# A two-layer decoder step: its head by halves of the weight units, and the second layer's gate on two pairs of banks

## The chip, the cores and the metric

One core of one Trainium2 chip runs the whole program. The metric is the device time of one execution in microseconds (us), as the median of several runs. The profile is of one further execution.

## The reference

One inference step of a decoder with two layers, D_MODEL 1024, on 1024 prompt tokens and 32 sample tokens (8 sequences of 4), 1056 in all. All arithmetic is float32. What matters here:

```python
h = rms_norm(x, g);  z = h @ W_in                    # layer 0: 12 tiles of 128 columns, layer 1: 14
# layer 0: windowed attention (12 query heads, 4 kv heads); layer 1: gating in chunks of 128 tokens
u, v = split(gelu(z[:, :1536]));  vn = rms_norm(v, v_norm)
mixed = einsum('gij,ncjgd->ncigd', tril(W_s), vn) + b_s      # 4 groups of 192 columns
o = u * mixed
xo = memory_attention(rms_norm(z_q), mem_k, mem_v)   # both layers: 4 heads into 256 memory tokens
x = x + concat([o, xo]) @ W_out
x = x + (silu(causal_conv3(h2 @ W_g)) * (h2 @ W_u)) @ W_down    # h2 = rms_norm(x), D_FF 2816
```

## The kernel before

**Products.** Activations lie with features on the 128 partitions and the 1056 tokens along the free axis, in 3 chunks of 352 (`NCH`, `CH`). Each float32 product is made of three: a tensor is cut into a high part that TensorE reads at its fast float32 rate, and a low part that is the remainder. Per contraction tile k, `products` (L600 to L602) issues hi·hi, hi·lo and lo·hi. A weight **unit** is 128 x 1024 floats (512 KB), 8 tiles of k. It is loaded into `raw` by SyncE, ScalarE makes the high part `w_hi` (`high_front`, `high_up`, at L1150), and VectorE (`low_front`, L1650) or GpSimd (`low`, L468) makes the low part `w_lo`. A chunk of a unit is 24 matmuls and ends in `proj`. The chunks of even units go to banks 0 to 2 of PSUM, those of odd units to 3 to 5. Banks 6 and 7 are for small sums. Whoever reads a chunk out of PSUM counts up `freed[slot]`, on which TensorE waits before it overwrites the bank.

**The head** (layer 0, before the first attention). SyncE issues in this order (L416 to L426): unit 0, tiles 0 to 3 of x for chunk 0, the gains, tiles 4 to 7 of x for chunk 0, unit 1, all of x for chunk 1, all of x for chunk 2, ten small constants, the memory tokens, `sel_t`. The normalisation is applied behind the product: TensorE multiplies x times gain, and `rb`, the reciprocal root of the mean square of each token spread over all partitions, multiplies the result on its way out of PSUM (L2016). ScalarE makes `h_hi` (`high_of_h`, L1202) in 24 pieces e (chunk e//8, tile e%8), VectorE makes `h_lo` (L1610). `X_LANDS` names the pieces ahead of which both wait for a load of x. At piece 8 ScalarE waits for the load of chunk 1, and only then takes the high part of unit 1 (L1226 to L1230). Then ScalarE squares x in 24 instructions (L1234). TensorE (`front`, L702) makes the six chunks of units 0 and 1 in the order `FRONT_X`, with sums of squares (`x_squares`, L672) behind the fourth and the fifth. The square sum goes ScalarE root (L1188), VectorE reciprocal (L1615), TensorE spread by three small products (`norm_spread`, L650, banks 6 and 7, the third waits until `rb`'s first piece is out of bank 6), ScalarE copy to `rb`. Only then do the PSUM chunks of units 0 and 1 get read and scaled (L2016), and only then does unit 2 start. Units of the memory keys and values follow in `FRONT`, with their own normalisation (`mem_stat`, `mem_spread`, `add_mem_squares`).

**The gate** (layer 1, `gate`, L972; ScalarE L1542; VectorE L2060). It runs over 9 blocks: 32 sample tokens, then 8 chunks of 128. Per block TensorE turns the 6 tiles of vn to tokens on partitions (6 transposes, L985, into banks 0 and 1), ScalarE copies them to `vn_tok`, TensorE mixes (12 products, L1002 and L1005, into banks 2 and 3 or 4 and 5), VectorE adds the bias (L2067) and multiplies into u in `z` (L2070). TensorE's order is turn 0, turn 1, mix 0, turn 2, mix 1 and so on. There is one pair of banks for the turns, so turn n waits until ScalarE has taken turn n-1. Ahead of turn 0 TensorE waits until every column is normalised (`z_normed` 24). ScalarE's order ahead of its first copy is: high part of a weight unit, GELU of the last column tile (L1506), wait for `z_normed`, two DMA issues of the output `chunk_v` (L1538, L1539). Behind the gate TensorE waits for the last bias and then starts the memory attention (`prompt_attention`): scores (L890), on VectorE the row maximum (`top`, L1815), on ScalarE exp (L1340), and so on. VectorE first fills `q_pad` for the sample's queries (L1690). The sample's memory scores (L783) follow the first two prompt scores.

## Time and profile before

| | us |
|---|---|
| median of 3 runs | 2281.68 |
| lowest, highest | 2279.41, 2282.77 |
| the profiled execution | 2283.67 |
| its span in the trace | 2281.9 |
| mean granted TensorE clock in it | 0.996 |

A row of the timeline has the start, the duration, the engine, the line of the kernel, the instruction with its output and inputs, and in brackets how long the engine was idle before it and who released it. "x24" are that many instructions in a row. Durations of matmuls overlap, since they are pipelined, so the distance between starts is what counts. In the row of a stretch the granted clock is 1.00 for the full clock and 0.50 for half of it.

### The profile page before, as it was taken

Reading aid. Unit: us, or ns where it says so; the run is one execution under the profiler, and the core shown is the slowest. Engines: PE = TensorE matmul, PEld = TensorE weight load, DVE = VectorE, ACT = ScalarE, POOL = GpSimd, SP = SyncE. Lnnn points to the kernel's source line nnn. Section 1 sums busy time; section 2 is a strip of 40 time slices with the busy share of each in tenths; the row PEclk is TensorE's granted clock in tenths of the full one; section 3 lists DMA queues with packets and bytes.
Section 4 is the critical chain, followed back from the end, with each engine's and each line's share of the span. In section 5 each row is a group of like instructions: output and inputs, shape, how many; then the busy total and the mean of one; then the engine's idle time right before and its main releaser. Section 6 shows DMA issues by size and latency. Waiting matters only on the chain.

```text
span 2281.9 us, 38777 instructions
## 1 busy us (share of the span) xinstructions
PE 2249.3 (99%) x15074; PEld 2155.3 (94%) x15074; DVE 1126.9 (49%) x2138; ACT 663.8 (29%) x1214; POOL 552.6 (24%) x412
## 2 busy tenths in 40 slices
PE   8999999999999999999999999999999999999999
PEld 7987679999999999999999986999999999999999
DVE  5335671564454554444562236246454555454554
ACT  6323791422211222211252225243211122211121
POOL 0002453322211222211252222342211222211221
PEclk9999999999999999999999999999999999999999
DMA  4223001111111111111111121111110111111112
GB/s 170 84 101 135 22 5 47 38 56 56 46 37 37 46 55 55 43 39 37 46 51 51 47 93 37 41 46 56 50 43 28 46 55 55 46 38 36 46 55 89
DMA packets 39143, 123.39 MB, mean 54 GB/s; under 512 B 5296, under 2 KB 13456, under 8 KB 38256
## 3 DMA queue, kind: packets, MB, share of 16 engines
q1 hardware_dynamic: 34656, 112.75, 15.1%
q10 hardware_dynamic: 4400, 9.43, 1.1%
q8 instruction: 60, 0.98, 0.2%
q14 instruction: 27, 0.22, 0.0%
HBM read 115.57 MB, written 8.63 MB: 54 GB/s over the span
## 4 chain that ended last, share of the span: by engine, by line
PE 92%; DVE 3%; issue 2%; ACT 1%; POOL 1%; DMA 0%; SPq 0%; ACTq 0%; DVEq 0%; POOLq 0%
PE ps L600 28%; PE ps L601 28%; PE ps L602 28%; DVE h_lo L1610 1%; PE ps L890 1%; PE ps L923 1%; PE ps L904 1%; PE ps L1002 1%; PE ps L783 1%; ACT s_exp L1340 1%; DMA x<-in_x_t 0%; PE ps L752 0%; POOL w_lo L468 0%; PE ps L985 0%; PE ps L1005 0%
## 5 line engine op out<-in xcount | busy, mean ns | idle before, releaser
L600 PE MATMUL ps<-h_hi,w_hi 128*128 128x352 f32 x3120 | 1014.2, 325 | 12.3 <-DVE h_lo L1610 10.1
L601 PE MATMUL ps<-h_lo,w_hi 128*128 128x352 f32 x3120 | 1001.9, 321 | 0.0
L602 PE MATMUL ps<-h_hi,w_lo 128*128 128x352 f32 x3120 | 1001.3, 321 | 0.0
L468 POOL TENSOR_TENSOR w_lo<-raw,w_hi 128x1024 fp32r<-128x1024 f32 x118 | 299.6, 2539 | 1522.1 <-ACT w_hi L1150 1522.1
L600 PEld LDWEIGHTS ps<-h_hi,w_hi 128*128 128x128 f32 x3120 | 586.7, 188 | 33.4 <-issue 22.3
L601 PEld LDWEIGHTS ps<-h_lo,w_hi 128*128 128x128 f32 x3120 | 587.7, 188 | 0.0
L602 PEld LDWEIGHTS ps<-h_hi,w_lo 128*128 128x128 f32 x3120 | 586.2, 188 | 0.0
L1954 DVE TENSOR_TENSOR x<-x,ps 128x352 f32<-128x352 f32 x528 | 270.7, 520 | 170.7 <-PE ps L602 170.0
L600 PE MATMUL ps<-g_hi,d_hi 128*128 128x352 f32 x1056 | 340.2, 322 | 0.0
L601 PE MATMUL ps<-g_lo,d_hi 128*128 128x352 f32 x1056 | 339.9, 322 | 0.0
L602 PE MATMUL ps<-g_hi,d_lo 128*128 128x352 f32 x1056 | 339.7, 322 | 0.0
L1150 ACT ACTIVATE w_hi<-raw 128x1024 fp32r<-128x1024 f32 x138 | 145.1, 1052 | 424.3 <-PE ps L602 404.6
L602 PEld LDWEIGHTS ps<-g_hi,d_lo 128*128 128x128 f32 x1056 | 198.7, 188 | 0.0
L601 PEld LDWEIGHTS ps<-g_lo,d_hi 128*128 128x128 f32 x1056 | 198.4, 188 | 0.0
L600 PEld LDWEIGHTS ps<-g_hi,d_hi 128*128 128x128 f32 x1056 | 198.3, 188 | 0.0
L1150 ACT ACTIVATE g_hi<-g_f 128x352 fp32r<-128x352 f32 x132 | 64.1, 498 | 443.4 <-DVE g_f L1941 443.4
L1880 DVE SCALAR_TENSOR_TENSOR c_buf<-a_buf,conv_c,c_buf 128x1024 f32<-128x1024 f32 x88 | 152.4, 1731 | 3.9 <-issue 0.4
L1927 DVE TENSOR_TENSOR a_buf<-ps,rb 128x352 f32<-128x352 f32 x88 | 46.0, 524 | 210.6 <-PE ps L602 210.5
L1941 DVE TENSOR_TENSOR g_f<-c_buf,ps 128x352 f32<-128x352 f32 x132 | 66.5, 519 | 165.5 <-PE ps L602 163.3
L2016 DVE TENSOR_TENSOR z<-ps,rb 128x352 f32<-128x352 f32 x78 | 40.3, 524 | 178.2 <-PE ps L602 169.8
L1419 ACT ACTIVATE c_buf<-c_buf 128x1056 f32<-128x1056 f32 x44 | 47.5, 1079 | 264.0 <-DVE c_buf L1883 264.0
L468 POOL TENSOR_TENSOR d_lo<-raw,d_hi 128x1024 fp32r<-128x1024 f32 x44 | 106.2, 2413 | 64.6 <-ACT d_hi L1150 64.6
(189 smaller groups left out, 1692.3 us busy)
## 6 DMA issues: line engine op xcount, KB each, us to landing
raw<-in_w SPq DMA_DIRECT2D x182, 512.0 KB, 3.5
s_mk<-in_s_mk SPq DMA_DIRECT2D x2, 2048.0 KB, 9.0
s_mv<-in_s_mv SPq DMA_DIRECT2D x2, 2048.0 KB, 13.6
out_y<-x ACTq DMA_DIRECT2D x7, 528.0 KB
x<-in_x_t SPq DMA_DIRECT2D x2, 1408.0 KB, 11.6
x<-in_x_t SPq DMA_DIRECT2D x2, 704.0 KB, 5.7
mem_x<-in_mem_t SPq DMA_DIRECT2D x1, 1024.0 KB, 6.9
s_k<-in_s_k SPq DMA_DIRECT2D x2, 512.0 KB, 4.5
```

What stands on the lines that cost most here:

```text
L468: pool.tensor_tensor(lo, raw[:, slot], hi.bitcast(F32), ALU.subtract).then_inc(prepped, 1)
L600: pe.matmul(out, a, hi_x(k), start=(first and n == 0), stop=False)
L601: pe.matmul(out, a, lo_x(k), start=False, stop=False)
L602: ins = pe.matmul(out, b, hi_x(k), start=False, stop=(last and n == len(ks) - 1))
L783: mm = pe.matmul(out[32 * c:32 * c + 32], stationary[:, 32 * b:32 * b + 32], moving(b), start=first and par == 0, stop=last and par == 1, ...
L1150: return act.activation(out, in_, ACT.Copy)
L1419: act.activation(c_buf[:, s], c_buf[:, s], ACT.Silu).then_inc(silued[l], 1)
L1880: ins = STT(out=cp, in0=ab[:, 48 + j:48 + j + SEQ], scalar=cc[:, j:j + 1], in1=cp, op0=ALU.mult, op1=ALU.add)
L1927: ins = TT(ab[:, at:at + CH], ps[:, c, 0:CH], rb[:, c * CH:(c + 1) * CH], ALU.mult)
L1941: TT(g_f[:, c * CH:(c + 1) * CH], c_buf[:, s, c * CH:(c + 1) * CH], ps[:, 3 + c, 0:CH], ALU.mult).then_inc(freed[1], 1)
L1954: TT(xx, xx, ps[:, down_bank(q, last), 0:CH], ALU.add).then_inc(dn_added, 1)
L2016: TT(z[:, unit_tiles(l)[u], cs], ps[:, 3 * (u % 2) + c, 0:CH], rb[:, cs], ALU.mult) \
```

## The change

**Head.** The first unit is loaded, cut into high part and low part in two halves of 512 columns, each with semaphores of its own; the second unit is loaded whole and cut in halves. Chunk 0 of x comes as tiles 0 and 1, 2 and 3, 4 to 7. Unit 1's high part is taken ahead of the wait for x's chunk 1. ScalarE squares x in 8 instructions of 1056 columns. TensorE puts the sums of squares behind the fifth and the sixth chunk. VectorE copies the six chunks out of PSUM unscaled, into `z_sq` (`take_first`), so that unit 2 can start at once. The three spreads come behind the first chunk of unit 2, into banks 6, 7 and 5, without a wait between them. ScalarE copies them to `rb` behind all eight squares of the memory tokens, and VectorE scales units 0 and 1 from `z_sq` with two instructions of 1056 columns. `mem_stat` comes one chunk later.

**Gate.** The turns alternate between banks 0, 1 and 6, 7, so turn n waits for the copy of turn n-2. Turn 0 waits for `z_normed` 18 only. ScalarE's GELU of the last column tile moves behind the second copy, and the two DMA issues of `chunk_v` go to SyncE's queue, behind the sample's memory caches and ahead of the weight stream. `q_pad` is filled in the middle of the gate. The first prompt scores are issued ahead of the last mix. The row maxima of the first two stand around the last bias, and the wait for the last bias is moved from ahead of the scores to ahead of the first transposes of probabilities. Buffers are laid out anew, and ScalarE's first three exps wait for the gate's last steps.

```diff
-X_LANDS = [0, 4, 8, 16]
+X_LANDS = [0, 2, 4, 8, 16]
+FRONT_RB = [6, 7, 5]
...
-            load_front(0)
-            load_x(0, slice(0, KD // 2), 0)
+            first = d["w"][S_INA + unit_tiles(0)[0]]
+            sp.dma_start(raw[:, 0, 0:D_MODEL // 2], first[:, 0:D_MODEL // 2]).then_inc(first_landed, 16)
+            load_x(0, slice(0, 2), 0)
             sp.dma_start(gain[:, :, :], d["gain"]).then_inc(gain_landed, 16)
-            load_x(1, slice(KD // 2, KD), 0)
+            sp.dma_start(raw[:, 0, D_MODEL // 2:], first[:, D_MODEL // 2:]).then_inc(raw_landed[0], 16)
+            load_x(1, slice(2, 4), 0)
+            load_x(2, slice(4, KD), 0)
             load_front(1)
-            load_x(2, slice(0, KD), 1)
-            load_x(3, slice(0, KD), 2)
+            load_x(3, slice(0, KD), 1)
+            load_x(4, slice(0, KD), 2)
...
+            sp.wait_ge(mx[1]["z_normed"], 24)
+            sp.dma_start(o["chunk_p"], z[:, 6:12, T - BLOCK:T]).then_inc(outs, 16)
+            sp.dma_start(o["chunk_s"], z[:, 6:12, 0:TS]).then_inc(outs, 16)
             stream((S_OUTB + 2) // 2, N_STREAM // 2)
...
-                    pe.wait_ge(prepped, u + 1)
-                    chunk(u, u, c, range(KD), lambda k: pe.wait_ge(h_ready, KD * c + k + 1))
-                    if q == 3:
+                    def landed(k):
+                        if q < 2 and k == 0:
+                            pe.wait_ge(first_lo, u + 1)
+                        if q < 2 and k == KD // 2:
+                            pe.wait_ge(prepped, u + 1)
+                        pe.wait_ge(h_ready, KD * c + k + 1)
+
+                    chunk(u, u, c, range(KD), landed)
+                    if q == 4:
                         pe.wait_ge(consts, 16 * NCONST)
                         x_squares(range(0, 4))
-                    if q == 4:
+                    if q == 5:
                         x_squares(range(4, 8))
+
+            def front_spreads():
+
                 pe.wait_ge(consts2, 16)
+                pe.wait_ge(recip, 1)
+                pe.wait_ge(freed[1], 3)
                 for c in range(NCH):
-                    norm_spread(0, c)
+                    pe.matmul(ps[:, FRONT_RB[c], 0:CH], sel_t[32 * c:32 * c + 32, SEL_ALL, :],
+                              rstd[32 * c:32 * c + 32, :], start=True, stop=True).then_inc(spread, 1)
...
+            def gate(first_scores):
+                m = mx[1]
+                tiles = [("s", 0)] + [("p", b) for b in range(NB)]
+                pe.wait_ge(m["masked"], 2)
+                pe.wait_ge(freed[0], 3 * ((R_INB + IN_B) // 2))
+                for n in range(NB + 2):
+                    if n < 2:
+                        pe.wait_ge(m["z_normed"], 18 if n == 0 else 24)
+                    if n < NB + 1:
+                        kind, b = tiles[n]
+                        w = TS if kind == "s" else BLOCK
+                        t0 = 0 if kind == "s" else TS + b * BLOCK
+                        if n >= 2:
+                            pe.wait_ge(m["gate_taken"], n - 1)
+                        out = banks(6 * (n % 2), 2, 768)
+                        for t in range(6):
+                            mm = pe.transpose(out[0:w, t * P:(t + 1) * P], z[:, 6 + t, t0:t0 + w], ident[:, :])
+                        mm.then_inc(m["gate_turned"], 1)
...
+                        pe.wait_ge(m["gate_taken"], q + 1)
+                        if q >= 2:
+                            pe.wait_ge(m["gate_biased"], q - 1)
+                        if q == 0:
+                            pe.wait_ge(freed[1], 3 * ((R_INB + IN_B) // 2))
+                        if q == NB:
+                            first_scores()
+                        out = banks(4 - 2 * (q % 2), 2, 768)
...
+                    if n == 0 and l == 1:
+                        pe.wait_ge(m["gate_biased"], NB + 1)
...
+                if l == 1:
+                    gate(lambda: scores(0))
+                    pe.wait_ge(m["gate_biased"], NB)
                 for it in range(0 if l == 1 else 2, M + 2):
-                    if it < M:
+                    if it < M and (l == 0 or it > 0):
...
-                                if q == 2 and c == 1:
+                                if q == 2 and c == 0:
+                                    front_spreads()
+                                if q == 2 and c == 2:
                                     mem_stat()
...
-                if l == 1:
-                    pe.wait_ge(freed[0], 3 * ((R_INB + IN_B) // 2))
-                    pe.wait_ge(freed[1], 3 * ((R_INB + IN_B) // 2))
-
-                    pe.wait_ge(m["z_normed"], 24)
-                    gate()
-                if l == 1:
-
-                    pe.wait_ge(m["gate_biased"], NB + 1)
...
-                    scopy(rb[:, c * CH:(c + 1) * CH], ps[:, 6 + c % 2, 0:CH]).then_inc(rb_taken, 1)
+                    bank = FRONT_RB[c] if w == 0 else 6 + c % 2
+                    scopy(rb[:, c * CH:(c + 1) * CH], ps[:, bank, 0:CH]).then_inc(rb_taken, 1)
...
-            high_front(0)
+            act.wait_ge(first_landed, 16)
+            scopy(w_hi[:, 0, 0:D_MODEL // 2], raw[:, 0, 0:D_MODEL // 2]).then_inc(first_hi, 1)
             act.wait_ge(gain_landed, 16)
             for e in range(KD * NCH):
+                if e == 2:
+                    act.wait_ge(raw_landed[0], 16)
+                    scopy(w_hi[:, 0, D_MODEL // 2:], raw[:, 0, D_MODEL // 2:]).then_inc(hi_cut, 1)
+                if e == KD:
+                    act.wait_ge(raw_landed[1], 16)
+                    scopy(w_hi[:, 1, 0:D_MODEL // 2], raw[:, 1, 0:D_MODEL // 2]).then_inc(first_hi, 1)
+                    scopy(w_hi[:, 1, D_MODEL // 2:], raw[:, 1, D_MODEL // 2:]).then_inc(hi_cut, 1)
                 if e in X_LANDS:
                     act.wait_ge(x_landed[X_LANDS.index(e)], 16)
-                if e == KD:
-                    high_front(1)
                 high_of_h(0, e)
             for k in range(KD):
-                for c in range(NCH):
-                    cs = slice(c * CH, (c + 1) * CH)
-                    act.activation(x_sq[k // 4][:, k % 4, cs], x[:, k, cs], ACT.Square).then_inc(squared_x, 1)
+                act.activation(x_sq[k // 4][:, k % 4, :], x[:, k, :], ACT.Square).then_inc(squared_x, 1)
+            high_front(2)
             high_of_mem(0)
-            high_front(2)
...
-            norm_root(0, beside=lambda: mem_squares(range(0, 3)))
-            high_front(3)
-            mem_squares(range(3, KD))
+            def beside_root():
+
+                high_front(3)
+                mem_squares(range(0, KD))
+
+            norm_root(0, beside=beside_root)
...
+                    if l == 1 and n == 0:
+                        act.wait_ge(m["gate_mixed"], NB)
+                    if l == 1 and n in (1, 2):
+                        act.wait_ge(m["gate_mult"], NB + n - 1)
...
-                    act.wait_ge(freed[u % 2], 3 * (r // 2) + 3)
-                    if l == 1 and t < 12:
+                    if l == 0 and u < 2:
+                        act.wait_ge(first_scaled, u + 1)
+                    else:
+                        act.wait_ge(freed[u % 2], 3 * (r // 2) + 3)
+                    if l == 1 and t < 12 and u < IN_B - 1:
...
-                    act.wait_ge(m["z_normed"], 24)
-                    act.dma_start(o["chunk_p"], z[:, 6:12, T - BLOCK:T]).then_inc(outs, 16)
-                    act.dma_start(o["chunk_s"], z[:, 6:12, 0:TS]).then_inc(outs, 16)
...
-                        scopy(vn_tok[0:w, n % 2, :], banks(0, 2, 768)[0:w]).then_inc(m["gate_taken"], 1)
+                        scopy(vn_tok[0:w, n % 2, :], banks(6 * (n % 2), 2, 768)[0:w]).then_inc(m["gate_taken"], 1)
+                        if n == 1:
+                            t = unit_tiles(1)[IN_B - 1]
+                            act.activation(z[:, t, :], z[:, t, :], ACT.Gelu).then_inc(m["gelud"], 1)
...
-            low_front(0)
+            def take_first(q):
+
+                u, c = FRONT_X[q]
+                dve.wait_ge(proj, q + 1)
+                dve.tensor_copy(z_sq[:, u, c * CH:(c + 1) * CH], ps[:, 3 * u + c, 0:CH]).then_inc(freed[u], 1)
+
+            def first_half(u):
+
+                half = slice(0, D_MODEL // 2)
+                dve.wait_ge(first_hi, u + 1)
+                TT(w_lo[:, u, half], raw[:, u, half], w_hi[:, u, half].bitcast(F32), ALU.subtract).then_inc(first_lo, 1)
+
+            def second_half(u):
+
+                half = slice(D_MODEL // 2, D_MODEL)
+                dve.wait_ge(hi_cut, u + 1)
+                TT(w_lo[:, u, half], raw[:, u, half], w_hi[:, u, half].bitcast(F32), ALU.subtract).then_inc(prepped, 1)
+
+            first_half(0)
             dve.wait_ge(gain_landed, 16)
             for e in range(KD * NCH):
+                if e == 2:
+                    second_half(0)
+                if e == KD:
+                    first_half(1)
+                    second_half(1)
                 if e in X_LANDS:
                     dve.wait_ge(x_landed[X_LANDS.index(e)], 16)
-                if e == KD:
-                    low_front(1)
                 low_of_h(0, e)
+            for q in range(5):
+                take_first(q)
+            low_front(2)
             dve.wait_ge(mem_landed, 16)
             low_of_mem(0)
+            take_first(5)
...
+                def gate():
+
+                    def bias(q, w):
+
+                        mv = mixed[:, (q + 1) % 2, :].rearrange("p (t n) -> p t n", t=6)[:, :, 0:w]
+                        dve.wait_ge(m["gate_mixed"], q + 1)
+                        if q >= 2:
+                            dve.wait_ge(m["gate_mult"], q - 1)
+                        src = banks(4 - 2 * (q % 2), 2, 768).rearrange("p (t n) -> p t n", t=6)[:, :, 0:w]
+                        TT(mv, src, (bb4 if q == 0 else bb)[:, :, :], ALU.add).then_inc(m["gate_biased"], 1)
+
+                    def multiply(q, w):
+
+                        t0 = 0 if q == 0 else TS + (q - 1) * BLOCK
+                        mv = mixed[:, (q + 1) % 2, :].rearrange("p (t n) -> p t n", t=6)[:, :, 0:w]
+                        dve.wait_ge(m["gate_biased"], q + 1)
+                        zz = z[:, 0:6, t0:t0 + w]
+                        TT(zz, mv, zz, ALU.mult).then_inc(m["gate_mult"], 1)
+
+                    dve.wait_ge(m["gate_in"], 16 * 4)
+                    dve.wait_ge(m["gelud"], 12)
+                    for q in range(NB + 1):
+                        w = TS if q == 0 else BLOCK
+                        if q == NB // 2:
+                            dve.wait_ge(m["qpad_zeroed"], 1)
+                            fill(1, 0, lambda i: 12 + i).then_inc(m["qpad_filled"], 1)
+                        if q == NB:
+                            top(0)
+                        bias(q, w)
+                        if q == NB:
+                            top(1)
+                        multiply(q, w)
...
-                    low_front(2)
                     dve.wait_ge(neg, 4)
                 norm_rstd(2 * l)
+                if l == 0:
+                    add_mem_squares()
+                    low_front(3)
...
+                    if l == 0 and u < 2:
+                        dve.wait_ge(rb_taken, NCH)
+                        TT(z[:, unit_tiles(0)[u], :], z_sq[:, u, :], rb[:, :], ALU.mult).then_inc(first_scaled, 1)
                     for c in range(NCH):
+                        if l == 0 and u < 2:
+                            continue
...
-                        if l == 0 and u == 2 and c == 1:
+                        if l == 0 and u == 2 and c == 2:
...
-                    if l == 0 and 1 <= n < len(FRONT) - 2:
+                    if l == 0 and 2 <= n < len(FRONT) - 2:
                         low_front(n + 2)
-                    if l == 0 and u == 1:
-                        add_mem_squares()
```

## Rows read from the trace of the kernel before

**Rows 1.** The page, part 1: busy time of each engine, share, instructions.
```profile
PE 2249.3 (99%) x15074; PEld 2155.3 (94%) x15074; DVE 1126.9 (49%) x2138; ACT 663.8 (29%) x1214; POOL 552.6 (24%) x412
```

**Rows 2.** Timeline, TensorE, first 50 us: start, duration, engine, line, instruction, [idle before <-releaser].
```profile
8.12 0.63 PE L600 MATMUL ps<-h_hi,w_hi 128*128 128x352 f32 x1 [8.12 <-DVE h_lo L1610]
...
15.89 0.43 PE L600 MATMUL ps<-h_hi,w_hi 128*128 128x352 f32 x1 [1.24 <-DVE w_lo L1650]
...
34.05 2.57 PE L672 MATMUL ps<-x_sq,sel 128*32 128x352 f32 x24
...
41.15 0.86 PE L650 MATMUL ps<-rstd,sel_t 32*128 32x352 f32 x4 [0.52 <-DVE rstd L1615]
...
42.62 0.82 PE L650 MATMUL ps<-rstd,sel_t 32*128 32x352 f32 x2 [0.61 <-ACT rb L1150]
...
43.38 0.43 PE L600 MATMUL ps<-h_hi,w_hi 128*128 128x352 f32 x1
```

**Rows 3.** Timeline, ScalarE and VectorE, first 51 us.
```profile
6.65 3.94 ACT L1202 ACTIVATE h_hi<-x,gain 128x352 fp32r<-128x352 f32 x8 [1.03 <-DMA gain<-in_gain]
...
13.45 1.06 ACT L1150 ACTIVATE w_hi<-raw 128x1024 fp32r<-128x1024 f32 x1 [2.85 <-DMA x<-in_x_t]
...
46.92 3.60 DVE L1631 TENSOR_TENSOR mem_ssq<-mem_ssq,mem_sq 128x256 f32<-128x256 f32 x7
```

**Rows 4.** Chosen stretches: each engine's busy us (count), TensorE clock granted, DMA share, GB/s.
```profile
core 0: us, PE busy (x) PEld busy (x) DVE busy (x) ACT busy (x) POOL busy (x), PEclk, DMA share, GB/s
8.20:13.40 5.20, 5.20 (x18) 5.20 (x19) 3.25 (x7) 2.39 (x5) 0.00 (x0) 1.00 1.04 383
36.70:40.00 3.30, 3.30 (x22) 3.30 (x23) 1.52 (x2) 2.75 (x5) 0.00 (x0) 1.00 0.52 159
44.30:47.50 3.20, 3.20 (x12) 3.20 (x12) 3.10 (x7) 0.72 (x2) 0.00 (x0) 0.50 0.02 5
1358.80:1361.70 2.90, 1.57 (x8) 0.71 (x8) 1.11 (x2) 2.03 (x2) 1.69 (x1) 1.00 0.70 181
1362.90:1375.30 12.40, 12.40 (x59) 10.09 (x60) 2.63 (x4) 2.43 (x3) 1.88 (x2) 0.50 0.97 381
1367.20:1372.00 4.80, 4.80 (x23) 3.69 (x23) 0.71 (x2) 0.81 (x1) 0.00 (x0) 0.50 0.98 403
1379.00:1381.60 2.60, 2.60 (x23) 2.02 (x22) 1.92 (x2) 0.81 (x1) 0.00 (x0) 1.00 0.00 0
1395.90:1399.30 3.40, 2.20 (x36) 0.70 (x28) 2.18 (x6) 2.71 (x13) 1.98 (x5) 1.00 0.00 0
```

**Rows 5.** Timeline, TensorE, the second layer's gate and the first scores after it.
```profile
1360.44 0.81 PE L985 MATMUL ps<-ident,z 128*32 128x128 f32 x6 [0.88 <-DVE z L2035]
...
1362.85 1.54 PE L985 MATMUL ps<-ident,z 128*128 128x128 f32 x6 [1.60 <-ACT vn_tok L1150]
...
1364.33 0.63 PE L1002 MATMUL ps<-ws,vn_tok 32*128 32x32 f32 x2
...
1367.14 1.54 PE L985 MATMUL ps<-ident,z 128*128 128x128 f32 x6
...
1392.88 1.09 PE L890 MATMUL ps<-mem_k,z 64*64 64x256 f32 x16 [1.05 <-DVE mixed L2067]
...
1398.92 0.66 PE L890 MATMUL ps<-mem_k,z 64*64 64x256 f32 x8 [1.04 <-ACT s_exp L1340]
```

**Rows 6.** Timeline, ScalarE and VectorE, the same stretch.
```profile
1360.91 1.04 ACTq L1539 DMA_DIRECT2D out_chunk_s<-z  x1
...
1362.00 0.80 ACT L1150 ACTIVATE vn_tok<-ps 32x768 f32<-32x768 f32 x1 [1.10 <-PE ps L985]
...
1391.87 0.96 DVE L2067 TENSOR_TENSOR mixed<-ps,bb 128x768 f32<-128x768 f32 x1
...
1394.50 1.29 DVE L1815 TENSOR_REDUCE stat<-ps 128x2 f32<-128x512 f32 x2
...
1395.23 0.47 ACT L1340 ACTIVATE s_exp<-ps,stat 128x256 f32<-128x256 f32 x1 [5.29 <-DVE stat L1815]
```

100 lines of the change are left out of this document (36 added, 64 removed).

## The prediction

> **What bounds the kernel now.** The page first: TensorE is busy for 99% of the span, VectorE for half of it [rows 1]. So a change pays only where TensorE stands idle, where it runs at half its clock, or where it is given less to do. The change gives it the same products. The question is how many us of idling and of half clock lie in the two stretches it touches, and I read the timeline of TensorE there, with the releaser of each idle time, and then the granted clock by stretches.
>
> In the head TensorE first works at 8.12 us, waits 1.24 us for the low part of unit 1, 0.52 us for the reciprocal root and 0.61 us for the copy of `rb` [rows 2]. Matmuls are slow until about 13.5 us: 18 in 5.2 us, where 22 fit into 3.3 us later. The clock column prints 1.00 there, but the matmuls show the half clock. The slow pace comes back behind the two waits for `rb`: 12 matmuls in 3.2 us at a granted 0.50, from about 44.2 to 47.6 us [rows 4].
>
> In the gate TensorE waits 0.88 us and 1.60 us ahead of the first two turns and 1.05 us behind the last mix, later 1.04 us for an exp [rows 5]. From 1362.9 to 1375.3 us it never pauses, at a granted 0.50 (1.2 GHz). The same 23 matmuls take 4.8 us at that level and 2.6 us at 1.00 (2.4 GHz) [rows 4]: 46% of such time is lost, 5.7 us of the 12.4.
>
> **The head, step by step.**
>
> 1. Start. ScalarE's first `h_hi` waits for the gains, landed at 6.65 us [rows 3], behind 512 + 704 + 24 KB. Now 256 + 352 + 24 KB are ahead, 608 KB less. At the 383 GB/s of the first stretch [rows 4] that is 1.6 us. The extra issues on SyncE stay ahead of the data. Bounds: 1.0 us if the smaller loads pay more, 2.0 if the first data come no later. I take 1.7: the half unit's cut (half of what a whole one takes) ends before the gains land. Tiles 4 to 7 land when they did, but TensorE needs them only after four tiles at the slow pace, 3.5 us later.
> 2. Unit 1. Its high part began at 13.45 us, behind the wait for x's chunk 1 [rows 3], though the weights had been issued ahead of that. Now it follows piece 7, at about 10.5 us, and its first half is ready near 11.8 us, while chunk 0 ends at 12.7 (a start of 6.4 plus the 6.3 to 6.5 us it took). The 1.24 us go. Chunk 1 of x keeps its landing, and `h_lo` stays ahead of TensorE.
> 3. Squares. The second block of sums moves behind the sixth chunk. ScalarE's eight wide squares end earlier than 24 narrow ones, so the block waits for nothing. From its end (34.05 + 2.57 = 36.62 us) to the first spread were 4.53 us [rows 2]: table, root, reciprocal. They now lie beside the first chunk of unit 2, 24 matmuls, some 3.9 us at the pace of 22 records in 3.3 us with a few missing [rows 4]. So the wait of about 0.5 us stays. The three spreads took 2.23 us with the wait in them (41.15 to 43.38 us); back to back 1.25. With the copy's latency this gives 1.0 us.
> 4. Clock. One wait of 0.5 us in place of two, and a whole dense chunk ahead of it. I take it that the fall at 44.2 us goes: (3.2 us less 12 matmuls at the full pace, 1.8) is 1.4, with the edges 1.5 us. It is 0 if the fall stays.
> 5. What waits for `rb` now: VectorE's seven adds take 3.6 us behind the reciprocal [rows 3], ScalarE's `rb` copies come behind the squares, then unit 3's low part, two wide scalings (1.3 us each), the square of unit 0's tile. That ends some 7 us after the spreads begin. TensorE needs it after 1.25 us of spreads and two chunks of 3.8 us, near 9 us. The cover is 1.8 us; without it the loss is one for one. The six copies of `take_first` sit in VectorE's idle time.
>
> Head: 1.7 + 1.24 + 1.0 + 1.5 = 5.4 us, between 3.3 (no clock, poor start) and 6.6.
>
> **The gate, step by step.**
>
> 6. Entry. Turn 0 starts 0.88 us earlier, turn 1 right behind it in its own banks. ScalarE copies at once, since the GELU and two DMA issues (the second ends at 1361.95 us [rows 6]) are out of its way. Turn 0 at 1359.56, turned by 1360.3, copied by 1361.2 (0.80 us [rows 6]): mix 0 starts at 1361.2 in place of 1364.33 us [rows 5]. 3.1 us.
> 7. Mix 0 took 2.8 us at half clock (1364.33 to 1367.14) [rows 5]; at the full clock about 1.5. 1.3 us.
> 8. The next two blocks took 4.9 and 4.2 us until the clock was back; at full clock 2.7 each. 3.7 us. The six behind them are already bound by TensorE [rows 4] and gain nothing from the second pair of banks.
> 9. Tail. From the end of the last mix (1391.8) to the fifth scores (1398.92 us [rows 5]) were 7.1 us: bias, scores, `q_pad`, maxima, exps in series. Now the first scores (0.55 us) are issued ahead of the last mix and `q_pad` is filled. What remains behind the mix is bias 0.96, a maximum 0.65, multiply 0.96, the sample's maximum and the third one (together 1.1), two exps 0.9 [rows 6], 4.9 us with gaps. 7.1 less 5.4 is 1.7 us.
> 10. The GELU, now behind the second copy, ends near 1363.1 us, as mix 0 does, so the first bias hardly waits. The two output issues on SyncE's queue, 1.7 us by ScalarE's rows, put off the weight stream behind them; those units are first used after the attention, some 60 us later: nothing. Exps behind `gate_mult` are in the sum.
>
> Gate: 3.1 + 1.3 + 3.7 + 1.7 = 9.8 us if the clock does not fall.
>
> **The sum.** 5.4 + 9.8 = 15.2 us off the profiled execution's 2283.67, which is 2268.5. That execution is 2.0 us above the median of the runs shown (2281.68) and 0.9 above their highest; I put that down to the program's own spread, of which the after-kernel has its share, and subtract from the median. **2266.5 us**.
>
> **The doubtful term is the clock at the gate's entry.** It fell at 1361.8 us after a stretch with 1.57 us of work in 2.9, mostly small. Against that, it stayed at 1.00 through 1395.9 to 1399.3 us with 2.2 busy in 3.4 [rows 4]. Now the entry has idle time of only some 0.4 us, but its work is 32-row products and turns. The rows of full clock from 1379.0 hold a turn in each block, so turns and mixes keep the clock once it is up. The Trainium skill, TensorE: Matmul & The Clock Gate, section "Part 4: PE-mode transpose", says that the full clock does not engage for transposes, as they do not count as busy in the same way. By that rule two turns and a mix of 32 tokens in a row would pull the clock down here as before. The trace agrees in that the clock stayed low through mixes and turns for 12.4 us, and disagrees in that it rose among them.
>
> **Rivals.**
>
> A. As summed: 2266.5. Chance 0.44.
>
> B. The clock falls at the gate's entry all the same. From the rows the low spell costs 46% of its length: 1.5 us if it is as short as that in the head, 5.7 if as long as before. With 3 us, 2269.5. Chance 0.29. For it: what the entry consists of. Against: the idle time is gone.
>
> C. The clock in the head still falls behind the spreads, which are the thinnest work there: 2268.0. Chance 0.12.
>
> D. The halves bring nothing, since gains and first tiles land as before; the rest holds: 2268.2. Chance 0.04.
>
> E. The chain behind `rb` (step 5) or ScalarE's order makes a new wait, half of the gain is gone: 2274. Chance 0.04.
>
> F. The edits don't do what they say, because the waits were covering each other: 2280. Chance 0.04.
>
> G. Slower: the clock falls at the gate's entry and does not come back in it. The 22 us of work there then take 0.85 us more per us, 19 us: mix 8 ends, with the tail's 1.7 us taken off, 9 us later than in the trace. With ten us of attention at that level, 8.5 more, less the head's 5.4: 2294. It decides from 23 us of low work on (15.2 + 4.6 us lost). For it: low for 12.4 us without a pause. Against: the rise came in blocks of the same kind. Chance 0.03.
>
> **How the numbers follow.** A measurement of this kernel tells 0.2%, 4.6 us, from no change. A to E are faster by more, 0.93; F is the same, 0.04; G is slower, 0.03. The range takes in A to D with the bounds of the start and of the low spell: 15.2 + 1.2 (start and first slow spell better than taken), and some run to run spread, gives 2262 below; 5.4 and 9.8 less 2.0 and 5.7 give 2274, of which I leave out the last us: 2273.
>
> **What would show it.** In the profile after: the first matmul near 6.4 us; no wait of TensorE for `w_lo` of unit 1; one wait of about 0.5 us ahead of three spreads; granted clock 1.00 behind them. In the gate: turns 0 and 1 back to back, mix 0 about 1.7 us behind the start of turn 0, blocks of 2.7 us from the first on, and 29.5 us from turn 0 to the fifth scores where there were 39.4 from 1359.56. Wrong would be: a granted 0.50 after the entry (B), a wait on `z_sq` or `rb` behind unit 2 (E), a span shorter by under 5 us (F).

## The result and the profile after

| | before | after |
|---|---|---|
| median | 2281.96 (4 runs) | 2269.66 (4 runs) |
| lowest, highest | 2279.41, 2282.77 | 2268.05, 2270.59 |
| profiled execution | 2283.67 | 2269.62 |
| its span | 2281.9 | 2267.9 |
| mean granted clock in it | 0.996 | 0.998 |

After to before is 0.9947 (0.9936 to 0.9959), so the change takes off 12.3 us. The direction and the range were right; 15.2 us had been forecast. The time itself, 2269.66, lies next to rival B's 2269.5 and 3.2 us above the likeliest case's 2266.5, but that is a coincidence: the profile shows the gate at the full clock, as case A has it, and two sizes in the sum were off (below). The two profiled spans differ by 14.0 us. That is not the same number, and the difference between the two is half of what there is to learn here.

Part 1 of the page of the kernel after, to be held against [rows 1]: TensorE has the same 15074 instructions and is busy 6.7 us less, so about half of the 14.0 us was not idling but matmuls that ran at half clock.

```profile
PE 2242.6 (99%) x15074; PEld 2149.9 (95%) x15074; DVE 1129.0 (50%) x2142; ACT 662.8 (29%) x1200; POOL 552.4 (24%) x412
```

**The head.** Timeline of TensorE, first 50 us, only rows with a wait, for [rows 2].

```profile
6.29 0.63 PE L613 MATMUL ps<-h_hi,w_hi 128*128 128x352 f32 x1 [6.29 <-DVE h_lo L1655]
...
9.92 0.66 PE L613 MATMUL ps<-h_hi,w_hi 128*128 128x352 f32 x1 [1.54 <-DVE h_lo L1655]
...
43.73 0.87 PE L738 MATMUL ps<-rstd,sel_t 32*128 32x352 f32 x6 [0.47 <-issue]
```

The first matmul comes 1.83 us earlier, unit 1's wait for its low part is gone, and the three spreads stand in one row behind one wait. But there is a new wait of 1.54 us inside the first chunk, for tile 2 of x. ScalarE's timeline shows where it comes from, for [rows 3]. Its rows tell when ScalarE took a load up, which is no earlier than its landing.

```profile
3.38 0.63 ACT L1180 ACTIVATE w_hi<-raw 128x512 fp32r<-128x512 f32 x1 [1.27 <-DMA raw<-in_w]
4.81 1.07 ACT L1233 ACTIVATE h_hi<-x,gain 128x352 fp32r<-128x352 f32 x2 [0.81 <-DMA gain<-in_gain]
6.12 0.63 ACT L1180 ACTIVATE w_hi<-raw 128x512 fp32r<-128x512 f32 x1 [0.24 <-DMA raw<-in_w]
8.59 1.07 ACT L1233 ACTIVATE h_hi<-x,gain 128x352 fp32r<-128x352 f32 x2 [1.84 <-DMA x<-in_x_t]
10.37 2.02 ACT L1233 ACTIVATE h_hi<-x,gain 128x352 fp32r<-128x352 f32 x4 [0.71 <-DMA x<-in_x_t]
12.31 1.13 ACT L1180 ACTIVATE w_hi<-raw 128x512 fp32r<-128x512 f32 x2
15.29 4.91 ACT L1233 ACTIVATE h_hi<-x,gain 128x352 fp32r<-128x352 f32 x10 [1.85 <-DMA x<-in_x_t]
```

Tiles 2 and 3 are taken up at 8.59 us, tiles 4 to 7 at 10.37, chunk 1 at 15.29, where it had been 13.45. In the kernel before, the eight tiles of chunk 0 ran without a wait from 6.65 us on, so everything behind the split loads is late. The stretches show the rate, for both kernels (first after, then before, columns as in [rows 4]).

```profile
5.00:6.00 1.00, 0.00 (x0) 0.00 (x0) 0.45 (x1) 0.88 (x2) 0.00 (x0) 1.00 0.81 209
6.00:7.00 1.00, 0.71 (x2) 0.74 (x3) 0.85 (x3) 0.63 (x1) 0.00 (x0) 1.00 0.95 311
```

```profile
5.00:6.00 1.00, 0.00 (x0) 0.00 (x0) 0.35 (x1) 0.62 (x1) 0.00 (x0) 1.00 1.03 347
6.00:7.00 1.00, 0.00 (x0) 0.00 (x0) 0.88 (x1) 0.35 (x1) 0.00 (x0) 1.00 1.06 369
```

From 5 to 7 us the split loads move 520 KB where the wide ones moved 716 KB.

**The gate.** Timeline of TensorE, for [rows 5].

```profile
1354.65 1.62 PE L907 MATMUL ps<-ident,z 128*32 128x128 f32 x12
1356.43 0.40 PE L928 MATMUL ps<-ws,vn_tok 32*128 32x32 f32 x2 [0.16 <-ACT vn_tok L1180]
...
1358.12 0.87 PE L907 MATMUL ps<-ident,z 128*128 128x128 f32 x6
...
1360.85 0.82 PE L907 MATMUL ps<-ident,z 128*128 128x128 f32 x6
...
1363.53 0.82 PE L907 MATMUL ps<-ident,z 128*128 128x128 f32 x6
...
1379.82 0.66 PE L959 MATMUL ps<-mem_k,z 64*64 64x256 f32 x8
1380.41 1.93 PE L808 MATMUL ps<-s_mk,q_pad 128*32 128x256 f32 x32
1382.27 1.09 PE L959 MATMUL ps<-mem_k,z 64*64 64x256 f32 x16
1384.80 0.66 PE L959 MATMUL ps<-mem_k,z 64*64 64x256 f32 x8 [1.43 <-ACT s_exp L1382]
```

Turns 0 and 1 are one row of twelve. Mix 0 begins 1.78 us behind turn 0, and from there the turns come 2.7 us apart. From turn 0 to the fifth scores it takes 30.15 us, where it took 39.36. For the kernel before this is counted from 1359.56 us, the start of the 0.88 us that it waited ahead of turn 0; the kernels with the gate's edits don't wait there. The stretches say why, against the 0.50 of [rows 4]:

```profile
1356.40:1358.10 1.70, 1.67 (x16) 1.49 (x16) 0.00 (x0) 1.69 (x2) 1.70 (x2) 1.00 0.99 395
1358.10:1363.50 5.40, 5.40 (x45) 4.21 (x45) 2.63 (x4) 1.62 (x2) 1.83 (x2) 1.00 1.01 434
```

The granted clock stays at 1.00. In the kernel before it was at 0.50 for 3.4 us from 44.2 us, for 3.4 us in the first layer's attention and for 13.7 us from 1361.8 us. After, one such stretch is left, in the first layer's attention, and it is longer, some 6.8 us. The prediction had not looked there. It doesn't show in the time between the two parts: from VectorE's first reading of unit 3 to turn 0 it was 1290.0 us before and is 1289.6 us after.

### The profile page after: what moved, and what is told of

Its sections match the earlier page's. It is cut to its first block, busy times and chain, and to the rows that moved or that the text cites. A ratio compares the mean times of both kernels' runs of the same rounds, so it can differ in the third digit from the quotient of the medians.

```text
span 2267.9 us, 38768 instructions
## 1 busy us (share of the span) xinstructions
PE 2242.6 (99%) x15074; PEld 2149.9 (95%) x15074; DVE 1129.0 (50%) x2142; ACT 662.8 (29%) x1200; POOL 552.4 (24%) x412
## 4 chain that ended last, share of the span: by engine, by line
PE 94%; DVE 3%; ACT 1%; issue 1%; POOL 0%; DMA 0%; SPq 0%; ACTq 0%; DVEq 0%; POOLq 0%
PE ps L613 29%; PE ps L614 28%; PE ps L615 28%; DVE h_lo L1655 2%; PE ps L959 1%; PE ps L994 1%; PE ps L975 1%; PE ps L808 1%; PE ps L928 1%; ACT s_exp L1382 1%; PE ps L777 0%; PE ps L796 0%; PE ps L931 0%; DMA x<-in_x_t 0%; PE ps L907 0%
## 5 line engine op out<-in xcount | busy, mean ns | idle before, releaser
L1180 ACT ACTIVATE w_hi<-raw 128x1024 fp32r<-128x1024 f32 (+1 forms) x140 | 145.3, 1040 | 417.0 <-PE ps L615 403.2
```

The lines of the kernel that those rows point to most:

```text
L1180: return act.activation(out, in_, ACT.Copy)
```

## Experiments

Each kernel is the kernel after with the edit shown, except for the first two. All times are medians. The kernel before had 2280.85 us beside the first four, 2281.13 beside the next four and 2281.55 beside the last four.

**1 and 2. Each half by itself**

`gate_only` is the kernel before with the gate's part of the diff, `head_only` with the head's part.

```diff
-                        out = banks(0, 2, 768)
+                        out = banks(6 * (n % 2), 2, 768)
...
-                    act.wait_ge(m["z_normed"], 24)
-                    act.dma_start(o["chunk_p"], z[:, 6:12, T - BLOCK:T]).then_inc(outs, 16)
...
```

```diff
-X_LANDS = [0, 4, 8, 16]
+X_LANDS = [0, 2, 4, 8, 16]
+FRONT_RB = [6, 7, 5]
...
```

> The kernel before with the gate's part of the change alone (layout of its buffers, two pairs of banks for the turns, GELU and output issues moved, first scores and maxima in the last block). The profiled executions of before and after put 9.3 us on this part (14.1 us at the fifth scores less 4.85 at the entry). Theory 1, the two parts are independent and the profiled execution of before is a usual one: 2281.96 less 9.3, 2272.7 us, granted clock 1.00 from the entry on. Theory 2, the low clock of 12.4 us in the gate of before was a bad draw, and the median execution of before has less of it: 2274 to 2275. Rival: the head's shift sets where the clock falls, and without it the clock falls at the entry again: 2276 to 2278, with turns of 1.5 us in the gate.

> The kernel before with the head's part of the change alone. The profiled executions put 4.5 us on it at the third unit and after. Theory 1: 2281.96 less 4.5, 2277.5 us, the gate as in the trace of before with the low clock. Rival: less than 3 us (over 2279), since what the head gives is taken back by a longer low clock at the start of the first attention, which lasted 6.8 us after the change and 3.4 us before it.

`gate_only`: 2275.59 us, ratio 0.9975 (0.9965 to 0.9985), 5.3 us off. `head_only`: 2276.45 us, 0.9979 (0.9969 to 0.9989), 4.4 us off. The sum is 9.7; together they gave 12.3. With some 2.3 us either way on each, the three don't contradict one another. `head_only` is as its first theory had it, `gate_only` lies between its second theory and the rival. The head gives about what it gives in the whole change (4.5 us by the traces). The gate gives less than its traced 9.2; the timeline and a stretch of `gate_only` show one reason.

```profile
1360.39 0.40 PE L910 MATMUL ps<-ws,vn_tok 32*128 32x32 f32 x2 [0.16 <-ACT vn_tok L1160]
...
1390.28 0.66 PE L941 MATMUL ps<-mem_k,z 64*64 64x256 f32 x8 [1.44 <-ACT s_exp L1354]
```

```profile
1362.60:1365.60 3.00, 3.00 (x16) 2.22 (x16) 0.40 (x2) 0.81 (x1) 1.30 (x2) 0.50 1.01 431
```

The entry has the same short wait as after, and still the clock was at 0.50 for 3.4 us behind it: rival B in its short form. Turn 0 to the fifth scores took 31.67 us, 1.5 more than after. The other reason lies in the kernel before. The runs of one kernel differ by how long the clock is low: `gate_only` ran in 2272.25 us at a mean clock of 1.000 and in 2278.32 at 0.996. The kernel before, over 18 runs, took 2277.3 to 2280.7 us at 0.998 to 0.999, 2280.3 to 2282.3 at 0.997 and 2282.6 to 2284.1 at 0.996. The profiled execution of before, 2283.67 at 0.996, was one of the long ones.

**3 to 5. How the first loads are cut**

`x_four` brings chunk 0 of x in two loads as before, and keeps the first unit in halves:

```diff
-X_LANDS = [0, 2, 4, 8, 16]
+X_LANDS = [0, 4, 8, 16]
-            load_x(0, slice(0, 2), 0)
+            load_x(0, slice(0, 4), 0)
...
-            load_x(1, slice(2, 4), 0)
-            load_x(2, slice(4, KD), 0)
+            load_x(1, slice(4, KD), 0)
```

`w_whole` brings the first unit in one load, and x as after:

```diff
-            sp.dma_start(raw[:, 0, 0:D_MODEL // 2], first[:, 0:D_MODEL // 2]).then_inc(first_landed, 16)
+            sp.dma_start(raw[:, 0, :], first).then_inc(raw_landed[0], 16)
...
-            act.wait_ge(first_landed, 16)
+            act.wait_ge(raw_landed[0], 16)
```

`loads_before` has both edits.

> The changed kernel with x's first chunk loaded as tiles 0 to 3 and 4 to 7 as before, the weight halves kept. Theory S (splitting x costs DMA rate, and tiles 2 and 3 wait behind the second weight half): tiles land at about 6.0 and 8.7 us, the first matmul comes near 7.2, the 1.54 us wait goes, x's chunk 1 lands near 13.6 in place of 15.3, and the time falls by 0.5 to 1.2 us against the changed kernel. Rival W (the weight halves cost the rate): chunk 1 of x still lands at 15 us or later, and the time is that of the changed kernel or up to 1 us more.

> The changed kernel with the first weight unit loaded whole (its high and low parts still cut in halves), x still in 2, 2 and 4 tiles. Theory S: the gains land 0.7 us later than 4.8, the first matmul near 7.0, tiles 2 and 3 still late (8.5), chunk 1 of x still at 15 us, time within 0.5 us of the changed kernel. Rival W: chunk 1 of x lands at 13.5, tiles 2 and 3 at 6.7, no wait behind the second tile, and the time falls by about 1 us.

> The changed kernel with the first loads as before: the first unit whole, chunk 0 of x in 4 and 4 tiles; the high and low parts are still cut in halves. If splitting loads costs about as much as it gives: the gains land at 6.5 us, the first matmul comes near 8.0 (6.3 with the split loads), no wait inside the first chunk, x's chunk 1 lands near 13.4, the first spread near 42.4, and the time is within 1 us of the changed kernel. If the earlier start is a real gain: the first spread near 44.5 us and 1 us or more slower than the changed kernel.

| | median | ratio | first matmul |
|---|---|---|---|
| `x_four` | 2268.91 | 0.9948 (0.9931 to 0.9964) | 7.46 |
| `w_whole` | 2268.74 | 0.9950 (0.9934 to 0.9967) | 7.01 |
| `loads_before` | 2268.54 | 0.9942 (0.9925 to 0.9959) | 8.29 |

TensorE of `loads_before`, all its waits in the first 50 us:

```profile
8.29 0.63 PE L611 MATMUL ps<-h_hi,w_hi 128*128 128x352 f32 x1 [8.29 <-DVE h_lo L1653]
...
43.05 0.87 PE L736 MATMUL ps<-rstd,sel_t 32*128 32x352 f32 x6 [0.47 <-issue]
```

It starts 2.0 us later than after, and its spreads come 0.7 us earlier. Its median isn't above that of the kernel after either. So the cutting of the loads, the first half of what the change did at the start, is worth nothing that shows. Either split seems enough to delay the loads: ScalarE took up chunk 1 at 14.46 us in `x_four` and at 14.56 in `w_whole`, against 13.3 to 14.2 in the four profiles with neither split and 14.4 to 15.3 in the eight with both. So neither theory S, which put the delay on the split of x, nor rival W, which put it on the weight halves, had it whole.

**6 to 8. The gate's edits undone one by one**

`entry_undone` puts GELU and output issues back on ScalarE, ahead of the first copy:

```diff
-                    if l == 1 and t < 12 and u < IN_B - 1:
+                    if l == 1 and t < 12:
...
+                    act.wait_ge(m["z_normed"], 24)
+                    act.dma_start(o["chunk_p"], z[:, 6:12, T - BLOCK:T]).then_inc(outs, 16)
+                    act.dma_start(o["chunk_s"], z[:, 6:12, 0:TS]).then_inc(outs, 16)
```

`one_pair` turns all tiles into banks 0 and 1:

```diff
-                        if n >= 2:
-                            pe.wait_ge(m["gate_taken"], n - 1)
-                        out = banks(6 * (n % 2), 2, 768)
+                        if n >= 1:
+                            pe.wait_ge(m["gate_taken"], n)
+                        out = banks(0, 2, 768)
```

`tail_undone` puts the first scores and both maxima behind the last bias:

```diff
-                    gate(lambda: scores(0))
-                    pe.wait_ge(m["gate_biased"], NB)
+                    gate(lambda: None)
+                    pe.wait_ge(m["gate_biased"], NB + 1)
```

> The changed kernel with ScalarE's order at the gate's entry as before: GELU of the last tile and the two output issues ahead of the first copy. Two pairs of banks and the early turns stay. Theory (idle time at the entry pulls the clock down): TensorE waits some 1 us for the first copy behind turns 0 and 1, the granted clock falls to 0.50 at the entry for 3 us or more in the profile, the time is 2 to 5 us over the changed kernel. Rival (only the idle time itself counts): 1.0 us over, no fall.

> The changed kernel with all turns in banks 0 and 1, turn n waiting for the copy of turn n-1. Theory: blocks behind the entry are bound by TensorE at 2.68 us as in the trace of before, so only the entry pays, some 0.8 us for turn 1; with a fall of the clock at the entry 1.5 us more. Rival: the second pair is worth 0.2 us in every block, 1.8 us and more.

> The changed kernel with the first scores and the first two maxima behind the gate's last bias, as before (the early fill of q_pad stays). Theory: 1.2 to 1.7 us over the changed kernel, the distance from the end of the last mix to the fifth scores near 6.5 us where it is 5.1. Rival: the sample's maximum and the sums behind it set the pace anyway, under 0.5 us.

| | median | ratio | turn 0 to fifth scores |
|---|---|---|---|
| after | 2269.66 | 0.9947 | 30.15 |
| `entry_undone` | 2271.90 | 0.9953 (0.9937 to 0.9970) | 36.02 |
| `one_pair` | 2269.19 | 0.9950 (0.9933 to 0.9966) | 31.02 |
| `tail_undone` | 2269.66 | 0.9955 (0.9938 to 0.9971) | 30.92 |

`entry_undone`, timeline and stretches of TensorE:

```profile
1352.40 1.62 PE L904 MATMUL ps<-ident,z 128*32 128x128 f32 x12
1355.58 0.40 PE L925 MATMUL ps<-ws,vn_tok 32*128 32x32 f32 x2 [1.56 <-ACT vn_tok L1177]
...
1358.17 1.54 PE L904 MATMUL ps<-ident,z 128*128 128x128 f32 x6
...
1367.15 0.82 PE L904 MATMUL ps<-ident,z 128*128 128x128 f32 x6
```

```profile
1356.60:1366.20 9.60, 9.60 (x47) 7.75 (x47) 2.63 (x4) 1.62 (x2) 1.08 (x1) 0.50 0.99 409
```

The wait ahead of mix 0 is 1.56 us in place of 0.16, and the clock is at 0.50 for some 10 us behind it. The stretch costs 36.02 less 30.15, that is 5.9 us: 1.4 of waiting and 4.5 of clock. By the medians the cost is 2.2 us; of its four runs one was at a mean clock of 0.997 (the profiled one, 2273.15 us) and two at 0.999 (2269.94 and 2271.23), so it looks as if the long spell comes in some executions and not in others; where the clock was low in a run without a profile isn't shown. The three profiles with ScalarE's old order at the entry do agree: 13.7 us of half clock in before, some 10 us in `head_only` and here. The stretch of `head_only`:

```profile
1357.60:1367.40 9.80, 9.80 (x49) 8.04 (x48) 1.89 (x4) 1.62 (x2) 1.27 (x2) 0.50 1.00 412
```

`one_pair`:

```profile
1353.39 0.83 PE L907 MATMUL ps<-ident,z 128*32 128x128 f32 x6
1355.27 0.85 PE L907 MATMUL ps<-ident,z 128*128 128x128 f32 x6 [1.04 <-ACT vn_tok L1180]
...
1357.73 0.87 PE L907 MATMUL ps<-ident,z 128*128 128x128 f32 x6
...
1360.46 0.82 PE L907 MATMUL ps<-ident,z 128*128 128x128 f32 x6
```

With one pair of banks turn 1 waits 1.04 us for the copy of turn 0. That is 0.87 us of the stretch, at the entry; the blocks behind are 2.7 us apart as with two pairs, and this profile shows no fall of the clock. The second pair is worth its 0.9 us at the entry and nothing inside the gate, as step 8 had it.

`tail_undone`:

```profile
1379.68 1.09 PE L959 MATMUL ps<-mem_k,z 64*64 64x256 f32 x16 [1.05 <-DVE mixed L1911]
1380.71 1.93 PE L808 MATMUL ps<-s_mk,q_pad 128*32 128x256 f32 x32
...
1385.10 0.66 PE L959 MATMUL ps<-mem_k,z 64*64 64x256 f32 x8 [1.20 <-ACT s_exp L1382]
```

The early scores and maxima are worth 0.8 us in the trace, between the theory and the rival. What is left of the tail's gain, 0.6 us, would be that of the early `q_pad`, which this kernel keeps; that wasn't tried by itself. Neither this nor `one_pair` can be told from after by its median. One of the four runs of `tail_undone` took 2275.45 us at a mean clock of 0.996, the others 2269.50 to 2269.75 at 0.999 to 1.000. So, by its mean clock, a long low spell, somewhere, also comes to a kernel whose entry is as short as that of after.

**9. The kernel after once more**, on the same chip as the three that follow, without an edit.

> The changed kernel again, unaltered, as the partner of the other runs of this call. If execution to execution differences of the clock and of the first landings set its spread, the median stays within 1 us of 2269.66, and the profile's first spread of the root lies anywhere from 42.2 to 44.4 us, as it did in four profiles with the same head.

2268.09 us (2267.70 to 2270.34), ratio 0.9947 (0.9933 to 0.9960).

```profile
6.20 0.63 PE L613 MATMUL ps<-h_hi,w_hi 128*128 128x352 f32 x1 [6.20 <-DVE h_lo L1655]
...
9.17 0.66 PE L613 MATMUL ps<-h_hi,w_hi 128*128 128x352 f32 x1 [0.87 <-DVE h_lo L1655]
...
42.77 0.87 PE L738 MATMUL ps<-rstd,sel_t 32*128 32x352 f32 x6 [0.47 <-issue]
```

The wait for tile 2 is there again, 0.87 us. The spreads come 0.96 us earlier than in the first profile of the same code. So a difference of a microsecond between two profiles of the head shows nothing by itself, and `loads_before` (2268.54) doesn't beat this kernel, it equals it. The median is 1.6 us below the 2269.66 of the same code, more than the 1 us that was expected, so a median of four or five runs doesn't settle a microsecond either.

**10. Unit 1's high part behind the wait for chunk 1**

```diff
+                if e in X_LANDS:
+                    act.wait_ge(x_landed[X_LANDS.index(e)], 16)
                 if e == KD:
...
-                if e in X_LANDS:
-                    act.wait_ge(x_landed[X_LANDS.index(e)], 16)
```

> The changed kernel with one thing undone: unit 1's high part is taken behind the wait for x's chunk 1, as before, in place of ahead of it. Theory: x's chunk 1 lands at 14.5 to 15.3 us, so the first half of unit 1 is ready near 16.3, while the first chunk ends near 14: a wait of 1 to 2 us for w_lo comes back, first spread 1 to 2 us later, time 1 to 2 us over the changed kernel. Rival: the pieces of chunk 1 set the pace anyway (they need the same wait), and it costs under 0.4 us.

2270.81 us, ratio 0.9954 (0.9940 to 0.9967), 2.7 us above `after_again`.

```profile
16.15 0.43 PE L613 MATMUL ps<-h_hi,w_hi 128*128 128x352 f32 x1 [1.03 <-DVE w_lo L1707]
```

The old wait is back, 1.03 us, and the spreads come at 45.19 us, 2.4 us later than in `after_again`. Of these 2.4 us the wait is 1.0. The rest is a first matmul at 6.67 us in place of 6.20 and a first chunk that ran at half pace to its end, and such differences come between profiles of one code too. The 2.7 us of the medians are as doubtful: against the first four runs of after (2269.66) they are 1.2, and the runs of this kernel (2269.04 to 2272.00) overlap with both. What the trace shows is a wait of 1 us that this order of ScalarE avoids; it is the only part of the start for which a run shows a gain.

**11. Sums and spreads one chunk earlier**

```diff
-                    if q == 4:
+                    if q == 3:
...
-                    if q == 5:
+                    if q == 4:
...
+                    front_spreads()
...
-                                if q == 2 and c == 0:
-                                    front_spreads()
```

> The changed kernel with the sums of squares behind the fourth and the fifth chunk and the three spreads ahead of unit 2, as before; the unscaled copies and the three separate banks stay. Theory: the cover of the root's chain is one chunk in both orders, so the wait stays 0.5 us, the spreads stay together at 0.8 us, and the time is within 0.5 us of the changed kernel; what the new order gives is only the separate bank. Rival: the copy of the sixth chunk out of bank 5 or the squares come late and TensorE waits 1 us or more.

2274.60 us, ratio 0.9971 (0.9960 to 0.9982), 6.5 us above `after_again`. My theory for this run missed and the rival was right. ScalarE's timeline, then a row and two stretches of TensorE's:

```profile
33.02 1.06 ACT L1179 ACTIVATE w_hi<-raw 128x1024 fp32r<-128x1024 f32 x1 [3.01 <-PE ps L615]
33.98 3.29 ACT L1250 ACTIVATE hm_hi<-mem_x,gain 128x256 fp32r<-128x256 f32 x8
37.29 1.28 ACT L1217 ACT_TABLE_LOAD   x1
38.59 0.55 ACT L1217 ACTIVATE root<-ps,cols 96x352 f32<-96x352 f32 x1
```

```profile
42.76 1.55 PE L738 MATMUL ps<-rstd,sel_t 32*128 32x352 f32 x6 [3.33 <-DVE rstd L1659]
```

```profile
42.70:49.20 6.50, 6.44 (x23) 5.50 (x24) 5.44 (x10) 3.45 (x9) 0.00 (x0) 0.50 0.06 11
49.90:52.00 2.10, 2.10 (x15) 2.10 (x14) 0.65 (x2) 1.17 (x2) 0.00 (x0) 1.00 0.28 113
```

The sums end at about 35.4 us here, but ScalarE cuts unit 2 and the memory tokens first and gets to the root only at 38.59. TensorE waits 3.33 us, and behind that wait the clock is at 0.50 for some 6.8 us: 23 matmuls in 6.5 us where `after_again` begins 22 in 3.5. The order of the change, a chunk of unit 2 ahead of the spreads, is worth 6.5 us in the presence of its other edits.

**12. The gains issued first**, on top of `loads_before`.

```diff
+            sp.dma_start(gain[:, :, :], d["gain"]).then_inc(gain_landed, 16)
+            first = d["w"][S_INA + unit_tiles(0)[0]]
...
-            sp.dma_start(gain[:, :, :], d["gain"]).then_inc(gain_landed, 16)
```

> The kernel of loads_before (first unit whole, x's chunk 0 in 4 and 4 tiles) with the gains issued ahead of all other loads. Theory: the pieces then wait for tiles 0 to 3 alone, which land 0.3 to 0.6 us ahead of the gains' 6.5, so the first matmul comes near 7.8 and the time is 0.3 us under that of loads_before, 2268.3. Rival: one more issue of 0.5 us ahead of the first unit delays all loads by that much: first matmul at 8.3 or later, no gain.

2268.74 us, ratio 0.9947 (0.9934 to 0.9961): nothing against `loads_before`. The rival was right: the first matmul comes at 9.00 us, since now the weights (5.63 us) and x (7.53 us) come last.

## Why the prediction was right, and where its sizes were off

Each term as forecast and as the two profiles have it. The head's whole is VectorE's reading of unit 3's first chunk, at 69.60 us before and 65.05 after; the gate's is turn 0 to the fifth scores. What isn't read from one place is the remainder of its part, and marked so.

| step | forecast | measured | from |
|---|---|---|---|
| 1 start | 1.7 | 0.0 | 48th recorded matmul at 19.66, then 18.46; 1.2 less is step 2's |
| 2 wait of unit 1 | 1.24 | 1.2 | the row is gone |
| 3 spreads | 1.0 | 1.5 | wait and spreads 2.75 us, then 1.27 |
| 4, 5 clock in the head | 1.5 | 1.8 | remainder of 4.5 |
| 6 entry | 3.1 | 3.0 | mix 0 behind turn 0: 4.77, then 1.78 |
| 7 mix 0 | 1.3 | 1.1 | 2.81, then 1.69 |
| 8 two blocks | 3.7 | 3.7 | 9.1, then 5.4 |
| 9 tail | 1.7 | 1.4 | remainder of 9.2 |
| sum | 15.2 | 13.7 | spans: 14.0 |

**Step 1 failed**, twice. It said "Tiles 4 to 7 land when they did, but TensorE needs them only after four tiles at the slow pace". They didn't land when they did, and it was tile 2 that came late, which the step had not priced: a 1.54 us wait (0.87 in `after_again`). And it counted an earlier start one for one, although an earlier paragraph says that matmuls are slow until 13.5 us. What is done earlier at that pace is worth half. The table has all profiles of the new head whose first chunks run in the same order, on all engines; "full pace" is the first matmul row shorter than 0.35 us.

| | first matmul | waits before full pace | full pace | spreads |
|---|---|---|---|---|
| after | 6.29 | 1.54 | 13.99 | 43.73 |
| `after_again` | 6.20 | 0.87 | 12.73 | 42.77 |
| `entry_undone` | 7.03 | 0 | 11.42 | 42.24 |
| `one_pair` | 6.78 | 0.18 | 11.37 | 42.42 |
| `tail_undone` | 6.44 | 0.97 | 15.23 | 44.40 |
| `head_only` | 6.28 | 0.74 | 12.58 | 42.78 |
| `w_whole` | 7.01 | 0.11 | 11.45 | 42.13 |
| `x_four` | 7.46 | 0 | 12.50 | 42.54 |
| `loads_before` | 8.29 | 0 | 12.50 | 43.05 |
| `gains_first` | 9.00 | 0 | 15.20 | 44.62 |

The spreads come at 32.8 us, plus half the moment of full pace, plus half of first matmul and waits; the ten rows keep to that within 0.5 us. The first six are one head code, and their moment of full pace lies anywhere from 11.4 to 15.2 us. Nothing that the change did at the start is as large as that. Rival D ("The halves bring nothing"), given 0.04, was right in what the halves gave, not in its reason: the gains did land earlier, and were taken up at 4.81 us in place of 6.65.

**The clock in the head (step 4)** came out as forecast, but in part by luck. `gate_only` runs the old head, with both waits ahead of and among the spreads (0.52 and 0.61 us), and in its profile the clock does not fall behind them:

```profile
44.30:47.50 3.20, 3.20 (x22) 3.20 (x22) 3.10 (x7) 0.72 (x2) 0.00 (x0) 1.00 0.00 0
```

That is 22 matmuls in the stretch where [rows 4] has 12 at 0.50. Unit 3's first chunk is read at 67.87 us there, 1.7 us ahead of the profile of before, while its spreads begin only 0.2 us earlier (40.98 and 41.15). So the old head loses some 1.5 us to the clock in some executions only, and against this one 2.8 of the head's 4.5 us are left. With the spreads behind a chunk of unit 2 none of eleven profiles shows the fall, so rival C did not come.

**The sum was set against the wrong base.** The prediction wrote: "I put that down to the program's own spread, of which the after-kernel has its share, and subtract from the median." The spread is not noise on top of the terms. In the kernel before it goes with the length of the low clock, and the terms 4 and 6 to 8 were read off an execution that had 3.4 us of it in the head and 13.7 us in the gate. The kernel after shows neither, and its profiled execution (2269.62) lies at its median while that of before lay 1.7 us above its own. 14.0 less 1.7 is 12.3. To be consistent, the terms should have come off 2283.67, which gives 2268.5, or the 5.7 us for the clock should have been taken at the middle of what executions show. The 2.9 us by which the forecast was too large are thus 1.7 of base and 1.2 of terms: 1.7 too much in step 1 and 0.6 in the gate, of which the spreads and what the table has no place for (0.3 us between unit 3 and the gate) gave some back.

**The clock at the entry** was named as the doubtful term, and rightly. Of eleven profiles with the gate's edits and without the 1.56 us wait (`one_pair` and `tail_undone` among them) nine show 1.00 throughout the gate, two (`gate_only`, `x_four`) 3.4 us of 0.50. Rival B is thus a matter of the execution: it is the rare case, and in the profiles in its short form (the run of `tail_undone` at 0.996 may have been a long one). Turns and mixes alone don't pull the clock down: in the second stretch of the gate above 12 of 45 matmuls are turns, all others mixes, and the clock is at 1.00. The Trainium skill, TensorE: Matmul & The Clock Gate, section "Part 4: PE-mode transpose", says that the full clock does not engage for transposes; it doesn't say what a mixture does. Here blocks with a turn of 0.82 us in 2.68 us keep the full clock, so the prediction's use of it, that the entry would pull the clock down, did not come true in nine of eleven profiles. Turns without mixes were not tried. What goes with the fall is idling amid small products: the entry's products are the same in `entry_undone`, and its wait ahead of mix 0 is 1.56 us in place of 0.16. Which of the waits before (0.88 us or 1.60 us) did it there wasn't tried singly, but `one_pair`, with 1.04 us in place of the second, kept the clock in its one profile.

**Steps 2, 5 to 8 and 10** held in the profiles; the first matmul at 6.29 us (6.4 forecast) and 30.15 us from turn 0 to the fifth scores (29.5) were as said. No wait on `z_sq` or `rb` shows up (E): TensorE waits 0.6 us for the low part of unit 3, as before. Step 3's wait of 0.47 us for a forecast 0.5 was right, and `spreads_early` shows what it stands on. Its spreads were 0.80 us for a forecast 1.25. F and G did not come.

**No version beat the kernel after.** `loads_before` equals it with two DMA issues less, and has the narrowest runs of all (2267.78 to 2268.87, clock 0.999 in each).

## What to carry to other kernels

Here an earlier start was worth only half while TensorE still ran at half clock, and splitting the first loads to get it delayed the loads behind them: price the loads behind the split as well as the split one. If part of a profiled time is low clock, ask how much of it the median execution has before taking it off the median: the mean clock listed with each run tells that. Look for a short wait among small products, in a chain that looks cheap: 1.4 us of waiting at the gate's entry cost 5.9 us in the profile and 2.2 by the medians.
